# A fused decoder layer: where the sparse heads' outputs are turned back and scaled

## What is computed

```
def masked_softmax(s, mask):
    s = jnp.where(mask, s, NEG)
    m = jnp.max(s, axis=-1, keepdims=True)
    p = jnp.where(mask, jnp.exp(s - m), 0.0)
    den = jnp.sum(p, axis=-1, keepdims=True)
    probs = p / jnp.maximum(den, 1e-30)
...
s_s = einsum('bghqd,bgqkd->bghqk', qc, k_sel) * scale + bias_s
p_s, _ = masked_softmax(s_s, (dist_s >= 0)[:, :, None])
o_s = einsum('bghqk,bgqkd->bghqd', p_s, v_sel)
...
o_w = einsum('bghqk,bgkd->bghqd', p_w, vwc)
return gc[..., 0:1] * o_c + gc[..., 1:2] * o_s + gc[..., 2:3] * o_w
```

## Time and profile before

| | us |
|---|---|
| median of 3 runs | 1146.07 |
| lowest, highest | 1146.03, 1146.32 |
| the profiled execution, its own time | 1146.04 |
| its span | 1144.2 |
| TensorE busy in the span | 1130.2 (99%) |
| weight loads busy | 990.4 (87%) |
| VectorE busy | 790.0 (69%) |
| ScalarE busy | 551.6 (48%) |
| GpSimd busy | 112.1 (10%) |

### The profile page before, as it was taken

One profiled execution on the slowest core, in us unless ns is written; L12 is line 12 of the kernel. 1 busy time (PEld: TensorE's weight loads), 2 busy tenths in 40 slices (PEclk: granted clock), 3 DMA queues, 4 the chain that ended last, 5 costly groups with the idle time before them and its releaser, 6 DMA issues.

```text
span 1144.2 us, 18877 instructions
## 1 busy us (share of the span) xinstructions
PE 1130.2 (99%) x7148; PEld 990.4 (87%) x7148; DVE 790.0 (69%) x1208; ACT 551.6 (48%) x1008; POOL 112.1 (10%) x222
## 2 busy tenths in 40 slices
PE   9999999999999999999999999999999999999997
PEld 7889999988887888887977888887889999998886
DVE  5888888855356365444878553698689888878863
ACT  6245555542225312245778422357445555556543
POOL 0000000056006030000001400002000000000002
PEclk9999999999999999999999999999999999999999
DMA  7313333365954697454200223344233333335541
GB/s 222 108 53 98 110 110 110 111 255 202 377 221 155 205 335 225 129 167 146 78 2 3 76 75 109 121 162 141 74 87 97 95 92 108 110 124 201 204 153 73
DMA packets 148430, 157.99 MB, mean 138 GB/s; under 512 B 4868, under 2 KB 125868, under 8 KB 146812
## 3 DMA queue, kind: packets, MB, share of 16 engines
q1 hardware_dynamic: 139184, 117.46, 33.2%
q0 software_dynamic: 9072, 39.66, 9.7%
q10 hardware_dynamic: 112, 0.03, 0.0%
HBM read 140.10 MB, written 21.49 MB: 141 GB/s over the span
## 4 chain that ended last, share of the span: by engine, by line
PE 96%; DVE 2%; ACT 1%; issue 1%; DVEq 0%; POOL 0%; ACTq 0%; POOLq 0%
PE ps L2188 28%; PE ps L2295 28%; PE ps L2328 10%; PE ps L2354 6%; PE ps L2483 4%; PE ps L2801 3%; PE ps L2373 3%; PE ps L2779 2%; PE ps L2614 1%; PE ps L2638 1%; PE ps L2767 1%; PE ps L2545 1%; PE ps L2584 1%; PE ps L2566 1%; PE ps L2555 1%
## 5 line engine op out<-in xcount | busy, mean ns | idle before, releaser
L1437 DVE TENSOR_TENSOR ring_lo<-ring_raw,ring_hi 128x2048 fp32r<-128x2048 f32 (+1 forms) x56 | 126.3, 2256 | 114.1 <-ACT ring_hi L937 114.1
L937 ACT ACTIVATE ring_hi<-ring_raw 128x2048 fp32r<-128x2048 f32 (+1 forms) x56 | 105.3, 1882 | 188.3 <-PE ps L2328 71.0
L2188 PE MATMUL ps<-xn_hi,ring_hi 128*128 128x512 f32 x472 | 186.1, 394 | 2.7 <-DVE xn_lo L1476 2.3
L2188 PE MATMUL ps<-xn_hi,ring_lo 128*128 128x512 f32 x472 | 183.9, 390 | 0.0
L2188 PE MATMUL ps<-xn_lo,ring_hi 128*128 128x512 f32 x472 | 183.7, 389 | 0.0
L2295 PE MATMUL ps<-s_hi,ring_hi 128*128 128x256 f32 x512 | 144.9, 283 | 0.0
L2295 PE MATMUL ps<-s_lo,ring_hi 128*128 128x256 f32 x512 | 144.9, 283 | 0.0
L2295 PE MATMUL ps<-s_hi,ring_lo 128*128 128x256 f32 x512 | 144.9, 283 | 0.0
L2295 PE MATMUL ps<-x_hi,ring_lo 128*128 128x256 f32 x384 | 108.7, 283 | 0.0
L2295 PE MATMUL ps<-x_lo,ring_hi 128*128 128x256 f32 x384 | 108.7, 283 | 0.0
L2295 PE MATMUL ps<-x_hi,ring_hi 128*128 128x256 f32 x384 | 108.7, 283 | 0.0
(11 more groups left out here) (389 smaller groups left out, 2386.0 us busy)
## 6 DMA issues: line engine op xcount, KB each, us to landing
ring_raw<-in_ffn_w_gu SPq DMA_DIRECT2D x86, 512.0 KB, 4.9
ring_raw<-in_w_in SPq DMA_DIRECT2D x42, 512.0 KB, 4.7
ring_raw<-in_ffn_w_down SPq DMA_DIRECT2D x40, 512.0 KB, 4.3
ring_raw<-weight_sums SPq DMA_DIRECT2D x24, 512.0 KB, 4.0
down_block<-in_ffn_w_down POOLq DMA_DIRECT2D x8, 1024.0 KB, 9.5
weight_sums<-down_block POOLq DMA_DIRECT2D x8, 1024.0 KB, 9.2
out_block<-in_w_out POOLq DMA_DIRECT2D x4, 1024.0 KB, 8.7
weight_sums<-out_block POOLq DMA_DIRECT2D x4, 1024.0 KB, 10.5
```

Of the source, the lines that this page charges most:

```text
L937: e = act.activation(dst, src, ACT.Copy)
L1437: e = dve.tensor_tensor(dst, src, f32(r), ALU.subtract)
L2188: e = pe.matmul(ps[:, 2 * (slot if pair is None else pair) + c, :], part(a, slot, k * 256 + c * P, P), xn[b][:, k, :], start=(k == 0 and i ...
```

## The change

It moves two calls and leaves every instruction as it is.

- In TensorE's loop the turn back of heads 0, 1 and 2 goes from the end of a round into the next round, behind that round's transposes and ahead of its scores (the round number in the test is raised by one for it).
- In VectorE's loop `take_branch` goes from the head of the round, ahead of the low copy, to behind the biases of the same round.

```
@@ VectorE, L2043 @@
-                for b, done in ((0, S_DONE), (1, W_DONE)):
-                    j, rest = divmod(pair - done - 4, 5)
-                    if rest == 0 and 0 <= j < HPG:
-                        take_branch(j, b)
                 if P0 < pair <= NP:
                     take_low_pT(pair - 1)
                 for u in (2 * pair + 2, 2 * pair + 3):
...
                     if u < NU:
                         add_bias(u)
+                for b, done in ((0, S_DONE), (1, W_DONE)):
+                    j, rest = divmod(pair - done - 4, 5)
+                    if rest == 0 and 0 <= j < HPG:
+                        take_branch(j, b)
@@ TensorE, L2703 @@
             for pair in range(P0 + 1, NP):
                 transposes_halved(pair - 1)
+                for b, done in ((0, S_DONE), (1, W_DONE)):
+                    j, rest = divmod(pair - done - 4, 5)
+                    if rest == 0 and 0 <= j < HPG - 1:
+                        turn_back(j, b)
                 if pair + 1 < NP:
                     scores(2 * pair + 2)
...
-                for b, done in ((0, S_DONE), (1, W_DONE)):
-                    j, rest = divmod(pair - done - 3, 5)
-                    if rest == 0 and 0 <= j < HPG - 1:
-                        turn_back(j, b)
```

## The result

The changed kernel takes 1149.90 us (median of 8 runs, 1149.09 to 1151.06) against 1146.24 us for the kernel before in the same comparison: ratio 1.0028, 95% interval 1.0020 to 1.0037. A second comparison of the same two gave 1149.41 us and 1.0031 (1.0021 to 1.0040). By the ratios it is 3.2 to 3.6 us slower; 2.9 was forecast. The forecast's range of 8 in 10 ended at 1149.7: the median of the first comparison lies 0.2 us above it, the one of the second within it. The narrower range of the forecast itself, to 1149.4, is missed by both.

A forecast was written before the change was run, and what follows sets the result against it. TensorE was taken to bound the sparse stretch. New waits of 2.3 and 1.35 us plus tile changes 0.7, less 1.4 of waits gone, gave about +2.9 on 1146.04: 1148.9 us, 8-in-10 range 1147.7 to 1149.7.

The forecast's parts named there:

- What bounds the kernel: Sparse pairs' stretch: TensorE, busy 59.75 of 61 us, sets the time; its delays and gains reach the end whole.
- What goes: Sparse stretch: two transposes' waits for high copies and three turns back's waits for `oT_sb` vanish, 1.4 us in all.
- Tile changes, 0.12 at each place: TensorE, six moved turns back: transposes into turn back 0.64, out to scores 0.58, adding 0.7 us in all.
- Values wait for the scaling: TensorE's values wait for VectorE's later scaling: 3 x 0.25, 2 x 0.26, and 1.0 in round 29; 2.3 us.
- Transposes wait for the high copy: TensorE's transposes, no longer behind the turn back, wait for ScalarE: 3 x 0.35 and 2 x 0.15, 1.35 us.
- The sum: Whole kernel: new waits and tile changes less waits gone and 0.03 for each of three waiting transposes, +2.9 us.
- more than summed: Turn back's way out costs another 0.12 per place, or later low copies delay ScalarE further: +3.6, 1149.6 us; chance 0.14.
- The rival of no loss: Sparse stretch: all waits go, 1144.6 to 1145.3 us; no loss or a gain up to 1.4 had chance 0.06.

The follow-up runs named there:

- VectorE's half alone: Against the kernel before, only VectorE's scaling (`take_branch`) moved behind the biases, TensorE's loop as before: 1148.33 us, ratio 1.0014.

## Why the prediction was right, and where its sums were small

- **What bounds the kernel.** Right. The delay of TensorE in the stretch reaches the end whole: 507.65 us follow in the kernel before, 507.53 in the changed one's second profile. The first gate product behind the loop starts at 636.10, where 635.9 was forecast and 632.96 was the start before; this profile comes to the stretch 0.23 earlier.
- **What goes.** Right: the waits for `oT_sb` and the two old waits for high copies are gone.
- **Tile changes, 0.12 at each place.** Right: transposes to turn back 0.64 (600.00 to 600.64), turn back to scores 0.59 (600.64 to 601.23), together 0.13 more than 0.58 and 0.52 before. The Trainium skill, "TensorEngine Tiling (Array Packing)", section Key Properties, says that changing the tiling mode drains the array. This trace agrees, with 0.12 as the price of one: transposes into scores of the same tile shape take 0.52, with one wait instruction ahead of the scores, and into the turn back 0.64, with one ahead of it too, so the wait instruction alone does not explain the 0.12. The turn back between scores and values, where the shape changes anyhow, shows no such price. The sum took off 0.09, 0.03 for each of three transposes that have waited. Into the turn back that does not show: the ones that waited take 0.64 (600.00 to 600.64), the others 0.64 too (593.76 to 594.40).
- **Values wait for the scaling: six waits, mechanism right, size small.** This is the mis-sized term: 3 x 0.25, 2 x 0.26 and 1.0 were put down, 2.3 in all. Start to start they are 0.35 (598.66 against 598.31; 605.05 against 603.83 + 0.87 = 604.70), five times, and 1.74 - 0.64 = 1.10 for the last: 2.85. Two latencies made most of it. The biases start 0.11 behind the values and not 0.07 (595.89 to 596.00), and the values start 0.15 behind the scaling's end (597.82 + 0.69 = 598.51 to 598.66), where 0.10 was taken. The 0.14 of the earlier trace rows with the earlier trace rows, at the upper end of the two that were weighed, lay nearest.
- **Transposes wait for the high copy: right, a little large.** 600.00 against 598.66 + 1.03 is 0.31, three times, and 0.11 (608.77 against 607.63 + 1.03), twice: 1.15, where 1.35 stood.
- **The sum.** 2.85 + 1.15 + 6 x 0.13 - 1.4 = 3.4, measured 3.37, forecast 2.9. The errors partly cancel: 0.6 too little for the values' waits, 0.1 for the tile changes and 0.1 taken off for the waited transposes, 0.2 too much for the high copies. That the first median lies just outside the wide range and the second just inside is chance of a few tenths. The rival "more than summed" (+3.6) came nearer in size, for a wrong cause: the way out of the turn back costs 0.59, as assumed, and ScalarE is not pushed back further, since the waits for the high copy are shorter than forecast.
- **The rival of no loss** needed all gaps closed; they stayed open by a little more than forecast. The first profile's +3.9 in the span (1144.2 to 1148.1) holds 0.8 behind the stretch that is not the change's.

## What to carry to other kernels

A wait of an engine with spare time is dear when other engines' inputs are queued behind it: here the places of a group of 1 us on VectorE and of four transposes on TensorE moved the stretch between +5.1, +3.4, +1.35 and -1.1 us, with not one instruction added. When a release is moved later, look for its consumer at the end of the loop, where the work that covered it in the other rounds is missing; that one place was a third of the loss. And give a step that changes the tile shape a place where the shape changes on both sides already.

## What the runs showed of the hardware

**A pause is followed by half clock in some executions.** At the start of the second feed-forward TensorE does 20 transposes (L2212) in 3.24 us and then waits 1.15 us for `xn_lo`. In the first profile of the kernel before it goes on at full clock; in the second, with the same instructions and the same 1.15, it does not (columns: length of the stretch, busy us of five engines, granted clock). First profile, then second:

```profile
799.00:803.00 4.00, 3.44 (x17) 2.84 (x18) 3.19 (x5) 3.75 (x5) 0.00 (x0) 1.00 0.00 0
```

```profile
799.00:803.00 4.00, 3.27 (x9) 2.61 (x10) 3.19 (x5) 3.36 (x5) 0.00 (x0) 0.61 0.00 0
```

The products behind the pause, first profile, then second:

```profile
799.87 0.40 PE L2188 MATMUL ps<-xn_lo,ring_hi 128*128 128x512 f32 x1
800.10 0.39 PE L2188 MATMUL ps<-xn_hi,ring_lo 128*128 128x512 f32 x1
```

```profile
799.73 0.64 PE L2188 MATMUL ps<-xn_hi,ring_hi 128*128 128x512 f32 x1 [1.15 <-DVE xn_lo L1476]
800.17 0.63 PE L2188 MATMUL ps<-xn_lo,ring_hi 128*128 128x512 f32 x1
```

The products come every 0.43 us, where the first profile has one every 0.23 at the full 2.4 GHz. That is the lower level of 1.2 GHz, for some three microseconds (granted 0.51 from 799.80 to 802.80). TensorE is 1.6 us later behind this place, and the part behind the stretch is as much longer (509.27 against 507.65). Three of the ten profiles have it: this one and both of the version with the turn back between scores and values (509.26 and 509.22). Whether that version calls it forth or had it twice by chance, these runs do not settle; the kernel before has it without any change. In the profiled executions it more than takes back the gain of 1.1 us. The clock of this place is known for those alone.

**A transfer that lands late.** In the out product ScalarE makes `third_hi` from a piece of `weight_sums`. It waits 0.2 us for that transfer in the first profile of the kernel before and 1.2 us in the first of the changed one:

```profile
ACT third_hi L1365 <- DMA ring_raw<-weight_sums: 0.2, 1, 0.2
```

```profile
ACT third_hi L1365 <- DMA ring_raw<-weight_sums: 1.2, 1, 1.2
PE ps L2801 <- ACT ps L1378: 0.6, 1, 0.6
```

From the start of the issues (766.13 and 769.28) to the copy (770.58 and 774.75) it is 4.45 and 5.47 us. In the second case TensorE then waits 0.6 us for L1378. The changed kernel's second profile has 4.41 us and no such wait of TensorE. VectorE's half alone has a shorter one (0.3). Why the transfer takes longer in some executions stays open, and so does whether the change makes that likelier: both profiles of the kernel before are without the wait of TensorE. This moves the time by up to 0.8 us from one execution to the next (508.41 against 507.53 behind the stretch), and the clock by 1.6: for a change of 1 us the repeatable stretch told more than the whole time did.
